# Writing out the up-projection of a convolutional feed-forward: one engine loop replaced by straight-line programs

## The reference

```python
h2 = rmsnorm(x, p['norm_ffn_g'])
up, ffn_buf = causal_dwconv(h2 @ p['ffn_w_up'], ffn_buf, p['ffn_conv_w'], p['ffn_conv_b'])
x = x + (jax.nn.silu(up[..., :D_FF]) * up[..., D_FF:]) @ p['ffn_w_down']
```

## Time and profile before

| | |
|---|---|
| median of 3 runs | 2947.7 us (2947.0 to 2960.29) |
| the profiled execution: span from first to last instruction | 2949.8 us |
| PE busy, share of the span | 2693.6 us, 91% |
| DVE busy | 1872.8 us, 63% |
| ACT busy | 1352.8 us, 46% |
| feed-forward of the first layer / of the second | 1238 to 1480 us / 2699 to 2940 us |

### The profile page before, as it was taken

One profiled execution on the slowest core, in us unless ns is written; L12 is line 12 of the kernel. 1 busy time (PEld: TensorE's weight loads), 2 busy tenths in 40 slices (PEclk: granted clock), 3 DMA queues, 4 the chain that ended last, 5 costly groups with the idle time before them and its releaser, 6 DMA issues. The chain is left out here.

```text
span 2949.8 us, 62087 instructions
## 1 busy us (share of the span) xinstructions
PE 2693.6 (91%) x24092; PEld 2462.7 (83%) x24092; DVE 1872.8 (63%) x3117; ACT 1352.8 (46%) x2294; POOL 841.2 (29%) x696
## 2 busy tenths in 40 slices
PE   7987889999999899899989878799999998998998
PEld 6876459999989689899978764599999895998998
DVE  4854457777766655489448454577777676554893
ACT  4733354545444244354357333555554442533542
POOL 0030009999910400000000300199999004000000
PEclk9999989999998999999989999899999998999999
DMA  5423459677545376365453243696866344764544
GB/s 134 110 59 105 138 100 148 117 129 122 83 79 161 97 202 168 104 166 139 126 115 101 65 132 112 115 141 115 139 106 104 74 141 124 199 172 108 161 133 120
DMA packets 838374, 365.86 MB, mean 124 GB/s; under 512 B 406189, under 2 KB 825558, under 8 KB 837512
## 3 DMA queue, kind: packets, MB, share of 16 engines
q1 hardware_dynamic: 835858, 360.77, 53.7%
q10 hardware_dynamic: 2232, 1.26, 0.2%
HBM read 342.63 MB, written 61.23 MB: 137 GB/s over the span
## 5 line engine op out<-in xcount | busy, mean ns | idle before, releaser
L1213 PE MATMUL key_banks<-w_kb_head,latent_T_head 128*128 128x352 f32 x1536 | 519.5, 338 | 9.7 <-DVE latent_T_rest L1341 9.7
L1213 PE MATMUL key_banks<-w_kb_head,latent_T_rest 128*128 128x352 f32 x1536 | 497.1, 324 | 0.0
L1213 PE MATMUL key_banks<-w_kb_rest,latent_T_head 128*128 128x352 f32 x1536 | 496.6, 323 | 0.0
L297 DVE TENSOR_TENSOR w_rests<-w_ring,w_heads 128x2048 fp32r<-128x2048 f32 (+1 forms) x150 | 321.6, 2147 | 146.9 <-ACT w_heads L291 146.7
L1355 DVE TENSOR_REDUCE w_kb<-key_sq 128x8 f32<-128x1024 f32 x256 | 311.2, 1216 | 12.4 <-ACT key_sq L1278 7.7
L1213 PEld LDWEIGHTS key_banks<-w_kb_head,latent_T_head 128*128 128x128 f32 x1536 | 290.5, 189 | 23.5 <-DVE latent_T_rest L1341 11.6
L1213 PEld LDWEIGHTS key_banks<-w_kb_rest,latent_T_head 128*128 128x128 f32 x1536 | 290.9, 189 | 0.0
L1213 PEld LDWEIGHTS key_banks<-w_kb_head,latent_T_rest 128*128 128x128 f32 x1536 | 289.8, 189 | 0.0
L291 ACT CAST w_heads<-w_ring 128x2048 fp32r<-128x2048 f32 (+1 forms) x150 | 268.4, 1792 | 42.8 <-ACT conv_last_rows L1934 19.7
L1033 POOL TENSOR_TENSOR rwkv_state_tmp<-rwkv_state,vec 128x1024 f32<-128x1024 f32 x64 | 153.3, 2395 | 455.6 <-POOLq L232 450.7
L1265 ACT CAST latent_T_head<-turn_bank 128x256 fp32r<-128x256 f32 x256 | 95.3, 372 | 400.6 <-PE key_banks L1217 392.2
(11 more groups left out here) (597 smaller groups left out, 7006.1 us busy)
## 6 DMA issues: line engine op xcount, KB each, us to landing
w_ring<-in_ffn_w_up_dram SPq DMA_DIRECT2D x88, 512.0 KB, 5.0
page_latents<-in_cache_kv_latent_dram SPq DMA_DIRECT2D x256, 128.0 KB, 2.4
latent_blocks<-page_latents SPq DMA_DIRECT2D x256, 128.0 KB, 3.9
latents<-page_latents SPq DMA_DIRECT2D x64, 512.0 KB, 8.4
w_ring<-in_w_in_dram SPq DMA_DIRECT2D x52, 512.0 KB, 3.8
w_ring<-in_w_gate_dram SPq DMA_DIRECT2D x46, 512.0 KB, 4.0
w_ring<-in_w_in_dram SPq DMA_DIRECT2D x20, 1024.0 KB, 5.9
w_ring<-in_ffn_w_down_dram SPq DMA_DIRECT2D x32, 384.0 KB, 3.3
```

Source lines behind the costliest of these rows:

```text
L297: ops.tensor_tensor(rests[:, slot, 0:tiles * P], ring[:, slot, 0:tiles * P], heads[:, slot, 0:tiles * P].bitcast(F32), ALU.subtract).then_ ...
L1213: last = nc.tensor.matmul(kbank[:, 3 * x + n, 0:KB], c[:, x, r * P:(r + 1) * P], w[:, r, cols], start=r == 0 and m == 0, stop=r == 1 and m ...
```

## The change

`rounds` no longer emits an engine loop: it calls the body 22 times with constant numbers for turn and slot. The four callers drop the engine argument. Units 3 to 17 are thereby written out on SP, PE, ACT and DVE like the units around them; operations, order, waits and buffers are the same. The loop over the two layers stays.

```diff
-def rounds(eng, n, ring, body):
+def rounds(n, ring, body):
 
 
-    full = n // ring
-    for r in range(min(ring, n)):
-        body(0, r, True)
-    if full > 2:
-        with eng.Fori(1, full - 1) as i:
-            for r in range(ring):
-                body(i, r, False)
-    if full > 1:
-        for r in range(ring):
-            body(full - 1, r, False)
-    if full:
-        for r in range(n - full * ring):
-            body(full, r, False)
+    for u in range(n):
+        body(u // ring, u % ring, u < ring)
...
-                rounds(sp, FT, RING, unit)
+                rounds(FT, RING, unit)
...
-                rounds(pe, FT, RING, unit)
+                rounds(FT, RING, unit)
...
-                rounds(act, FT, RING, unit)
+                rounds(FT, RING, unit)
...
-                rounds(dve, FT, RING, unit)
+                rounds(FT, RING, unit)
```

## The result

| | before | after |
|---|---|---|
| median of the runs | 2956.3 us (6 runs, 2947.0 to 2960.29) | 2939.2 us (6 runs, 2930.88 to 2946.39) |
| ratio after / before | | 0.9945, 95% interval 0.993 to 0.996 |
| profiled execution: its time / its span | - / 2949.8 us | 2940.14 / 2938.2 us |
| feed-forward, first layer | 241.61 us | 231.70 us |
| feed-forward, second layer | 238.78 us | 231.68 us |

A feed-forward is counted from the first square of its norm on ACT (L2053, after: L2042) to the start of the last addition to x on DVE (L2019, after: L2008).

The account below looks back on a forecast made before the run. PE and DVE were taken as close in the up-projection, DVE's 7.03 us a looped unit overtaking PE's 6.40. Gains of 9.70 us (first layer) and 6.95 (second), together 16.65, took 2947.7 to 2931.0 us, range 2925 to 2941.

Parts of the forecast that it names:

- first rival: Third down-projection tile: PE's wait stays or only shrinks; gain 7.74 us with wait and clock whole, 2940.0 us; chance 0.13.
- PE's late units: Up-projection units 12 to 21: PE no longer slowed to DVE's pace; gain 3.91 us first layer, 3.83 second.
- The wait at the third tile: Down-projection: PE's wait for DVE's rests of the third tile goes; gain 3.12 us in each layer.
- The cover: Third down-projection tile: ready 8.68 us after ACT's last copy, wanted by PE at 9.11, so 0.43 us to spare.
- The clock: Third down-projection tile, first layer: PE's clock no longer falls after the wait; gain 2.67 us, between 0 and 5.34.
- SP, PE and ACT at nothing: Up-projection: removing the loop's branch and register work on these three engines gains 0 us.
- Fetching at nothing: Up-projection: fetching the twelve more units written out on each of four engines costs 0 us.
- The absolute time: Whole kernel: the runs' median of 2947.7 us falls by 16.65 us to 2931.0 us.
- The profiled span: Whole profiled execution: its span of 2949.8 us falls to 2933.1 us.
- DVE did get faster: Denies a rival on DVE's up-projection units: space between operations is the engine's own, nothing moves, 2947.7 us; chance 0.09.
- nothing was slower: Denies a rival in the up-projection: instruction fetching holds PE, 46 us more, 2977 us; chance 0.04.

Follow-up runs that it names:

- after again: The changed kernel run once more, unaltered; 2937.03 us, ratio 0.9941 to before.
- only DVE: The kernel before with only DVE's up-projection units written out, SP, PE and ACT keeping their loops; 2938.06 us, ratio 0.9941 to before.
- the padded one: The changed kernel with two unused additions more on DVE in each of units 3 to 17, estimated at 0.80 us; 2953.27 us, ratio 0.9995 to before.
- the two partly looped kernels: The changed kernel with DVE's units 3 to 8, or 12 to 17, looped again; 2933.26 and 2944.42 us, one run each.
- the kernel with constant taps: The kernel before, loop kept, with the convolution's taps and biases read at constant addresses; 2946.31 us, one run, beside 2955.98 for before.

## Why the prediction was right

The time was given as 2931.0 us, range 2925 to 2941; measured were 2939.2. The gain was given as 16.65 us. By the traces the two stages of before add up to 480.4 to 480.7 us in five executions and those of after to 463.4 and 463.2 in two, a gain of about 17.3. By the runs, the eighteen with DVE written out (after, after again, only DVE) have a mean of 2938.0 (standard error 1.05) and the 29 of before one of 2955.0 (1.0): 17.0, with a standard error of 1.5.

The time alone could not have told the forecast from its first rival: 2939.2 lies nearer to that rival's 2940.0 than to 2931.0, and inside the range only because the range reached up to this rival's case. That is luck; the base was 8 us too low (see below), and it is the gain and the traces that decide for the forecast.

- *PE's late units, 3.91 and 3.83.* Right: 61.51 and 61.43 became 57.60. PE binds, DVE waits 0.19 us for ACT in the unit shown. That it is DVE's unit, and not some loop, was shown by the kernels with only DVE and all but DVE written out and by the padded one.
- *The wait at the third tile, 3.12 each.* Right in size: 3.48 became 0.36. The cover was too large on paper, 0.43 us, against 0.2 from the two partly looped kernels. The step that was off is when PE wants the tile: 9.11 us after the last copy was read from before, where PE's second tile had itself begun a little late (PE's weight load for it sat 0.19 us behind DVE's rests); in after it is 2860.89 - 2852.00 = 8.89. That 0.22 us a layer was gained too, beyond the forecast; the stages gained 0.15 and 0.21 more than forecast (7.10 for 6.95 in the second layer, 9.91 for 9.70 in the first), because the norm and the first units also moved by 0.1 to 0.2 us either way.
- *The clock, 2.67.* Right as taken, by five traces of before with one fall each. It was read from one trace and called the middle of 0 and 5.34; that four more would show the same share was not known then. The third tile took 4.45 and 4.44 us in after, at a granted clock of 1.00.
- *SP, PE and ACT at nothing.* Right, shown by the kernel with these three written out (1.0005), but for the open question of whether PE's loop has a part in the clock's fall.
- *Fetching at nothing.* Right. In 60 us of after's up-projection queue q8 brings four blocks where the loop needed one; PE is busy for all 59.00 and 60.00 us of the two stretches shown above. The DMA queue in after, 2741 to 2801 (packets, MB, share):

```profile
q8 instruction: 4, 0.07, 0.4%
```

The Trainium skill (Runtime: NRT & Kernel Launch, "Instruction fetch mechanics") holds that straight-line fetching is mostly hidden, and the trace agrees; it also holds that a taken branch stalls an engine for a fetch when its target isn't among the instructions held. The rows of DVE's loop show no such stall: the units at a turn's end are the shorter ones (L297 at 2793.00 to 2799.53, 6.53 us, against 6.71 ahead of it, in the kernel with constant taps). In the kernel before, from the second turn on, it is 6.95 to 6.98 against 7.02 to 7.04; the first turn's last unit takes 7.20, with a longer idle time (0.52 us) ahead of L1966 and none at the branch.

- *The absolute time.* 8 us too low, and that isn't a term of the sum: the base was. It was the median of three runs, 2947.7; 23 later ones have a median of 2955.9.
- *The profiled span,* given as 2933.1, was 2938.2. The stages did their part; the rest was in work that the change doesn't touch, and it was the trace of before that was out of the ordinary. The prompt's attention in the second layer is 152 matmuls in either kernel. Busy time and granted clock over it, after:

```profile
1845.20:1882.50 37.30, 35.46 (x152) 23.70 (x152) 21.71 (x75) 19.45 (x55) 0.00 (x0) 0.73 0.52 114
```

and before:

```profile
1854.50:1884.50 30.00, 26.43 (x152) 18.23 (x152) 21.48 (x75) 19.39 (x55) 0.00 (x0) 1.00 0.63 136
```

From its first matmul to its last it took 37.16 us after, with part of it at a clock of 0.50, and 29.93 in the first trace of before: 7.2 us, more than the 6.3 by which the whole stretch differs. In the four other traces of before it took 36.84, 35.59, 36.78 and 37.15 us, and in the first layer of the first trace 37.10; of the eight traces of other kernels one is short here too (all but DVE written out, 31.25), the rest took 36.77 to 37.16. So the span of 2949.8, from which the forecast was subtracted, came from an execution that was short in this place.

The rivals fell: DVE did get faster, the wait went altogether, and nothing was slower. The Trainium skill's rule on VectorE's drain (VectorE: DVE Perf Modes, "The DRAIN you can't avoid"), by which a semaphore after each operation costs nothing, isn't contradicted in the end: with constant addresses L1999 follows L1997 without idle time (2789.12 + 0.78 us, then 2789.93) even behind a wait on a register. What the loop put between these two was register work, which the rule doesn't speak of.

Open: the stretch between the stages was 1219.2 to 1229.8 us in the seven traces with DVE's whole loop left (the one with constant taps among them) and 1225.2 to 1230.8 in the six with it gone or partly gone. Whether the change shifts it by some us is not decided by so few; the gain by the runs, 17.0 with a standard error of 1.5 against 17.3 from the stages alone, speaks for no shift but would allow one of up to about 3 us.

## What to carry to other kernels

Here the engine loop cost time on one engine only, the one with the longest unit, whose instructions take addresses from registers; those of PE, ACT and SP cost nothing that the runs show. Compare that engine's unit inside the loop with a unit of the same code outside it (7.03 and 6.23 us), and with the unit of the engine next in line (6.40). The smaller of the two differences, 0.63 us, is a bound for each looped unit: 15 x 0.63 = 9.5 us a layer, of which 7.2 were gained (3.83 in the late units, 0.22 and 3.12 at the down-projection, second layer), because a lag that nobody waits for costs nothing. Look for where a lag is called in, here at the first work behind the loop that needs the last unit: six late units cost three times what six early ones did. Only DVE's program needed to be written out.

## What was not expected of the hardware

- Executions of one program differ by 9 to 23 us (2932.34 to 2941.09 in six runs of after, 2947.32 to 2965.32 in 23 of before, 2938.9 to 2962.31 in 14 with all but DVE written out). In the traces one such place is the same 152 small matmuls, 29.93 us at a granted clock of 1.00 and 37.16 where part of them ran at 0.50. Three runs gave a base 8 us off.
- After the same idle time of 2.9 us the granted clock fell in one layer and not in the other, in each of five executions of the same kernel, in the first layer twice and in the second three times; it fell after none of four such waits in the two kernels with a wait and PE written out, and never at that place after an idle time of 1.54 us or less (six waits).
- Register operations of 0.06 to 0.10 us on VectorE's sequencer were paid almost in full (0.38 of 0.44 us a unit), as time between the engine's operations.
